# Latent attention: twelve packed query tiles, rotary rows through GpSimd and DMA copies, takes moved within each head

## The reference

```python
def mla_queries(h, w_q_a, q_a_norm, w_q_b, q_nope_norm, q_rope_norm, cos, sin):
    c_q = rms_norm(h @ w_q_a, q_a_norm)                       # 384 wide
    q = (c_q @ w_q_b).reshape(bsz, seq, 16, 96)
    q_nope = rms_norm(q[..., :64], q_nope_norm)
    q_rope = apply_rope(rms_norm(q[..., 64:], q_rope_norm), cos, sin)   # 32 wide
    return concatenate([q_nope, q_rope])
# keys: k_nope = rms_norm of 64 columns of c_kv @ w_kv_b for each head, k_rope 32 wide, shared by all heads
# causal_block_attention: softmax(q k^T / sqrt(96)) v for 16 heads of 64 value columns; then x + o @ w_o
def apply_rope(x, cos, sin):
    x1, x2 = split(x, 2)
    return concatenate([x1 * cos - x2 * sin, x1 * sin + x2 * cos])
```

## Time and profile before

| what | value |
|---|---|
| median of three runs | 1870.35 us |
| the profiled execution | 1866.67 us, span 1864.6 us |
| PE busy | 1810.5 us (97%) |
| PE weight loads | 1395.1 us (75%), beside PE |
| DVE busy | 1041.5 us (56%) |
| ACT busy | 839.4 us (45%) |
| POOL busy | 199.6 us (11%) |
| mean granted TensorE clock | 0.99 |
| chain that ended last | PE 88%, DVE 4%, ACT 3%, POOL 3%, issue 1% |

### The profile page before, as it was taken

One profiled execution on the slowest core, in us unless ns is written; L12 is line 12 of the kernel. 1 busy time (PEld: TensorE's weight loads), 2 busy tenths in 40 slices (PEclk: granted clock), 3 DMA queues, 4 the chain that ended last, 5 costly groups with the idle time before them and its releaser, 6 DMA issues.

```text
span 1864.6 us, 24367 instructions
## 1 busy us (share of the span) xinstructions
PE 1810.5 (97%) x8934; PEld 1395.1 (75%) x8934; DVE 1041.5 (56%) x1633; ACT 839.4 (45%) x1406; POOL 199.6 (11%) x269
## 2 busy tenths in 40 slices
PE   9889999999999999999999999999999989999997
PEld 6677778888887766677888888768666767866675
DVE  8874454444334767755444434465555476556647
ACT  5423344443224666644444422232567633265753
POOL 7970000000000000000000000023000012200000
PEclk9989999999999999999999999999999999999998
DMA  6322322323333111122232333323111122311111
GB/s 212 103 58 79 98 94 90 101 91 98 94 96 101 44 35 28 62 74 96 90 101 92 98 94 94 97 87 106 57 57 46 46 90 88 105 51 52 57 45 57
DMA packets 58764, 152.21 MB, mean 82 GB/s; under 512 B 17152, under 2 KB 22048, under 8 KB 58672
## 3 DMA queue, kind: packets, MB, share of 16 engines
q1 hardware_dynamic: 55120, 148.27, 25.3%
q0 software_dynamic: 3552, 2.70, 0.5%
HBM read 143.79 MB, written 4.19 MB: 79 GB/s over the span
## 4 chain that ended last, share of the span: by engine, by line
PE 88%; DVE 4%; ACT 3%; POOL 3%; issue 1%; DMA 0%; SPq 0%; DVEq 0%; ACTq 0%; POOLq 0%
PE bank L2027 19%; PE bank L2028 18%; PE bank L2029 18%; PE bank L2522 3%; PE bank L2524 3%; PE bank L2523 3%; PE bank L2499 2%; PE bank L2487 2%; PE bank L2486 2%; PE bank L2485 2%; PE bank L2254 1%; PE bank L2282 1%; PE bank L2609 1%; PE bank L2537 1%; PE bank L2506 1%
## 5 line engine op out<-in xcount | busy, mean ns | idle before, releaser
L1253 DVE TENSOR_TENSOR wl<-raw,wh 128x1024 fp32r<-128x1024 f32 (+3 forms) x280 | 324.1, 1158 | 493.9 <-ACT wh L678 490.7
L678 ACT ACTIVATE wh<-raw 128x1024 fp32r<-128x1024 f32 (+3 forms) x280 | 279.2, 997 | 573.5 <-PE bank L2029 498.0
L2027 PE MATMUL bank<-xH,wh 128*128 128x512 f32 x904 | 355.2, 393 | 3.9 <-DVE wl L1253 2.1
L2029 PE MATMUL bank<-xH,wl 128*128 128x512 f32 x904 | 352.1, 389 | 0.0
L2028 PE MATMUL bank<-xL,wh 128*128 128x512 f32 x904 | 352.1, 389 | 0.0
L2027 PEld LDWEIGHTS bank<-xH,wh 128*128 128x128 f32 x904 | 169.9, 188 | 43.4 <-DVE xL L1259 3.2
L2028 PEld LDWEIGHTS bank<-xL,wh 128*128 128x128 f32 x904 | 170.0, 188 | 35.6 <-issue 1.0
L2029 PEld LDWEIGHTS bank<-xH,wl 128*128 128x128 f32 x904 | 169.8, 188 | 35.5
L2027 PE MATMUL bank<-hidH,wh 128*128 128x512 f32 x352 | 137.3, 390 | 0.0
L2029 PE MATMUL bank<-hidH,wl 128*128 128x512 f32 x352 | 136.9, 389 | 0.0
L2028 PE MATMUL bank<-hidL,wh 128*128 128x512 f32 x352 | 136.9, 389 | 0.0
(11 more groups left out here) (450 smaller groups left out, 3305.6 us busy)
## 6 DMA issues: line engine op xcount, KB each, us to landing
raw<-w_gu_dram SPq DMA_DIRECT2D x88, 512.0 KB, 3.3
raw<-w_p_dram SPq DMA_DIRECT2D x64, 512.0 KB, 3.4
raw<-w_dn_dram SPq DMA_DIRECT2D x32, 448.0 KB, 3.3
raw<-w_glu_dram SPq DMA_DIRECT2D x16, 512.0 KB, 3.5
raw<-w_dn_dram SPq DMA_DIRECT2D x16, 512.0 KB, 3.5
raw<-w_out_dram SPq DMA_DIRECT2D x16, 512.0 KB, 3.3
raw<-w_in_dram SPq DMA_DIRECT2D x8, 512.0 KB, 7.8
raw<-w_o_dram SPq DMA_DIRECT2D x8, 512.0 KB, 3.4
```

The source lines that it names most:

```text
L678: nc.scalar.activation(wh[:, (st.base + u) % 2, 0:kts * P], raw[:, (st.base + u) % 4, 0:kts * P], ACT.Copy).then_inc(w_high, 1)
L1253: nc.vector.tensor_tensor(wl[:, s, 0:kts * P], raw[:, (st.base + u) % 4, 0:kts * P], wh[:, s, 0:kts * P].bitcast(F32), ALU.subtract).then_ ...
L2027: nc.tensor.matmul(bank, wh[:, s, w], hi[:, k, :], start=first and kt == 0, stop=False)
L2029: ins = nc.tensor.matmul(bank, wl[:, s, w], hi[:, k, :], start=False, stop=last and kt == kts - 1)
```

## The change

The sixteen query tiles become twelve: eight tiles `("n", pair)` with the 64 nope rows of two heads, and four tiles `("r", g)` with the 32 rotary rows of four heads each. VectorE takes a rotary tile into `rope_q`; GpSimd has the two halves exchanged by two DMA copies into `rope_x`, multiplies both with tables (`qtab`, filled by sixteen DMA copies), adds them, and puts the 32 rows of each head into the four buffers `qst` by four DMA copies a pair. Buffers of queries are two pairs deep now; their unused rows are set to zero. The dictionaries `MAIN` and `SECOND` say which tile is projected in which head. The keys and the nope queries are taken behind `copy_turned` and ahead of the last `row_least` of a head, and the tile of `SECOND` (heads 0, 3 and 7) behind it. The blocks of output projection at the end are placed anew. `squares_of`, `root_of`, `projected`, `mean_square` and `take` are the old helpers for any tile, and `taken_from` gives a tile's bank and place in it. The masks of the mean matmul and the order of columns in the packed weights follow.

```diff
-BLOCKS_B = [("q", 0), ("k", 0), ("v", 0), ("v", 1), ("q", 1), ("k", 1)]
-for _p in range(1, NH // 2):
-    BLOCKS_B += [("q", 2 * _p), ("q", 2 * _p + 1)] + [("k", _p + 1)] * (_p + 1 < NH // 2)
+BLOCKS_B = [("r", 0), ("k", 0), ("v", 0), ("n", 0), ("v", 1), ("k", 1), ("n", 1), ("r", 1), ("n", 2), ("k", 2), ("r", 2),
+            ("n", 3), ("k", 3), ("n", 4), ("k", 4), ("r", 3), ("n", 5), ("k", 5), ("n", 6), ("k", 6), ("n", 7), ("k", 7)]
+IN_BANK2 = [("r", 0)] + [("n", p) for p in range(NH // 2)]
+IN_BANK3 = [b for b in BLOCKS_B if b[0] != "v" and b not in IN_BANK2]
+NORMED = [b for b in BLOCKS_B if b[0] != "v"]
+MAIN = dict(enumerate([(kind, p) for p in range(2, NH // 2) for kind in "nk"], 1))
+SECOND = {0: ("r", 1), 3: MAIN[3], 7: MAIN[7]}
+MAIN.update({3: ("r", 2), 7: ("r", 3)})
...
-    qst = [mla.tensor(f"qst{b}", [P, S]) for b in range(2)]
+    qst = [[mla.tensor(f"qst{s}", [P, S])[:, :] for s in range(2)], [sq[:, s, :] for s in range(2)]]
     qtab = [mla.tensor(f"qtab{s}", [P, S]) for s in range(2)]
+    rope_q, rope_x = T[:, 1, :], sd[:, :]
...
-            pool.wait_ge(sem("hid_used0"), 1)
             pool.dma_start(posI[:, :], pos.to_broadcast([P, S])).then_inc(sem("pos_loaded"), 16)
             pool.dma_start(means[:, :], con[:, CON["mean_even"][0]:CON["fold"][1]]).then_inc(sem("means_loaded"), 16)
+            pool.wait_ge(sem("rope_table"), 1)
+            for n in range(8):
+                to = slice(n * DR // 2, (n + 1) * DR // 2)
+                turning = DN + DR + n // 4 * DR // 2
+                pool.dma_start(qtab[0][to, :], ropeT[DN:DN + DR // 2, :]).then_inc(sem("rope_rows1"), 16)
+                pool.dma_start(qtab[1][to, :], ropeT[turning:turning + DR // 2, :]).then_inc(sem("rope_rows1"), 16)
+            pool.wait_ge(sem("latnorm_ready"), KQ + KKV)
+            pool.wait_ge(sem("latroot_ready"), 3)
+            for n in range(2):
+                nc.gpsimd.memset(qst[n][0][DN + DR:P, :], 0.0).then_inc(sem("latroot_ready"), 1)
+                nc.gpsimd.memset(qst[n][1][DR:DN, :], 0.0).then_inc(sem("latroot_ready"), 1)
+            pool.wait_ge(sem("latroot_ready"), 7)
+            for g in range(NH // 4):
+                pool.wait_ge(sem("roped"), 4 * g + 1)
+                for half in range(2):
+                    pool.dma_start(rope_x[half * DN:(half + 1) * DN, :], rope_q[(1 - half) * DN:(2 - half) * DN, :])\
+                        .then_inc(sem("rope_rows0"), 16)
+                if g == 0:
+                    pool.wait_ge(sem("rope_rows1"), 256)
+                pool.wait_ge(sem("rope_rows0"), 32 * (g + 1))
+                nc.gpsimd.tensor_tensor(rope_q, rope_q, qtab[0][:, :], ALU.mult).then_inc(sem("roped"), 1)
+                nc.gpsimd.tensor_tensor(rope_x, rope_x, qtab[1][:, :], ALU.mult).then_inc(sem("roped"), 1)
+                pool.wait_ge(sem("roped"), 4 * g + 3)
+                nc.gpsimd.tensor_tensor(rope_q, rope_q, rope_x, ALU.add).then_inc(sem("roped"), 1)
+                pool.wait_ge(sem("roped"), 4 * g + 4)
+                for pair in range(2 * g, 2 * g + 2):
+                    if pair >= 2:
+                        pool.wait_ge(sem("scores_ready"), 8 * pair - 8)
+                    for s in range(2):
+                        for half in range(2):
+                            to = (DN, 0)[s] + half * DR // 2
+                            at = half * DN + (2 * (pair % 2) + s) * DR // 2
+                            pool.dma_start(qst[pair % 2][s][to:to + DR // 2, :], rope_q[at:at + DR // 2, :])\
+                                .then_inc(sem(f"rope_placed{pair % 2}"), 16)
...
-                if h + 2 < NH:
-                    query_squares(h + 2)
-                    if h + 2 < NH - 2:
-                        ahead(st, 0, AT_B["q", h + 2], True)
+                if h in MAIN:
+                    squares_of(MAIN[h])
+                    if h < NH - 5:
+                        ahead(st, 0, AT_B[MAIN[h]], True)
                 for j in range(QT):
                     if j < 3:
                         copy_turned(h, j)
                     if h + 1 < NH:
                         probs(h + 1, 1 - s, j)
-                    if j == 1 and h + 2 < NH:
-                        query_root(h + 2)
-                        if s and pair + 2 < NH // 2:
-                            key_squares(pair + 2)
-                            ahead(st, 0, AT_B["k", pair + 2], True)
-                    if j == 2 and s and pair + 2 < NH // 2:
-                        key_root(pair + 2)
+                    if j == 1 and h in MAIN:
+                        root_of(MAIN[h])
+                    if j == 1 and h in SECOND:
+                        squares_of(SECOND[h])
+                        ahead(st, 0, AT_B[SECOND[h]], True)
+                    if j == 2 and h in SECOND:
+                        root_of(SECOND[h])
                 if pair and s == 0:
                     output_high(pair - 1)
-                if NH - 2 <= h + 2 < NH:
-                    ahead(st, 0, AT_B["q", h + 2], True)
+                if NH - 5 <= h < NH - 3:
+                    ahead(st, 0, AT_B[MAIN[h]], True)
...
+            def take_rope(g):
+                bank, i = taken_from(("r", g))
+                if g:
+                    for n in range(2):
+                        dve.wait_ge(sem(f"rope_placed{n}"), 64 * g)
+                dve.wait_ge(sem("rq_ready" if bank == 2 else "rk_ready"), i + 1)
+                nc.vector.scalar_tensor_tensor(rope_q, banks[bank][:, :], tiny[:, 25:26], (R if bank == 2 else acc)[:, :], ALU.mult, ALU.mult)\
+                    .then_inc(sem("roped"), 1)
+                dve.wait_ge(sem("roped"), 4 * g + 1)
+                dve.sem_inc(sem("q_used" if bank == 2 else "kv_used"), 1)
...
-            def head_queries(h):
-                s = h % 2
-                dve.wait_ge(sem("rq_ready"), h + 1)
-                step(nc.vector.tensor_tensor(qst[s][:, :], banks[2][:, :], R[:, :], ALU.mult))
+            def take_queries(pair):
+                dve.wait_ge(sem("rq_ready"), taken_from(("n", pair))[1] + 1)
+                for s, rows in enumerate((top, bottom)):
+                    step(nc.vector.scalar_tensor_tensor(qst[pair % 2][s][rows, :], banks[2][rows, :], tiny[rows, 24:25], R[rows, :],
+                                                        ALU.mult, ALU.mult))
                 dve.sem_inc(sem("q_used"), 1)
-                nc.vector.tensor_tensor(qst[s][:, :], qst[s][:, :], qtab[s][:, :], ALU.mult).then_inc(sem("qk_ready"), 1)
-
-            def head_keys(pair):
+                dve.sem_inc(sem("qk_ready"), 1)
+
+            def take_keys(pair):
...
-            head_queries(0)
-            head_keys(0)
+            take_keys(0)
             ahead(st, 0, 2, True)
+            ahead(st, 0, 3, True)
+            take_queries(0)
+            rope_rows(1)
             row_least(0, 0)
+            ahead(st, 0, 4, True)
             row_least(0, 1)
-            rope_rows(1)
-            ahead(st, 0, 3, True)
+            ahead(st, 0, 5, True)
             row_least(0, 2)
-            ahead(st, 0, 4, True)
+            ahead(st, 0, 6, True)
             share_first(0)
-            head_queries(1)
+            take_keys(1)
             row_least(0, 3)
-            ahead(st, 0, 5, True)
-            head_keys(1)
+            take_queries(1)
...
-                if h + 2 < NH - 2:
-                    ahead(st, 0, AT_B["q", h + 2], True)
-                elif NH - 2 <= h + 1 < NH:
-                    ahead(st, 0, AT_B["q", h + 1], True)
+                if h in MAIN and h < NH - 5:
+                    ahead(st, 0, AT_B[MAIN[h]], True)
+                elif NH - 4 <= h < NH - 2:
+                    ahead(st, 0, AT_B[MAIN[h - 1]], True)
                 if h + 1 < NH:
                     row_least(h + 1, 0)
                     row_least(h + 1, 1)
@@ -1716,17 +1782,17 @@
                 share_probs(h, 3)
                 if pair and s:
                     output_low(pair - 1)
-                if s == 0 and 1 <= pair < NH // 2 - 1:
-                    head_keys(pair + 1)
-                if h + 2 < NH:
-                    head_queries(h + 2)
-                if s and pair + 2 < NH // 2:
-                    ahead(st, 0, AT_B["k", pair + 2], True)
+                if h in SECOND:
+                    ahead(st, 0, AT_B[SECOND[h]], True)
                 if h + 1 < NH:
                     row_least(h + 1, 2)
                 copy_turned(h)
+                if h in MAIN:
+                    take(MAIN[h])
                 if h + 1 < NH:
                     row_least(h + 1, 3)
+                if h in SECOND:
+                    take(SECOND[h])
...
-                    pe.wait_ge(sem("qk_ready"), h + 1)
-                    pe.wait_ge(sem("kv_used"), pair + 2)
+                    pe.wait_ge(sem("qk_ready"), pair + 1)
+                    pe.wait_ge(sem(f"rope_placed{pair % 2}"), 64 * (pair // 2 + 1))
```

(68 more changed lines are left out.)

158 lines of the change are left out of this document (80 added, 78 removed).

## The result

The changed kernel takes 1875.97 us (median of 6 runs, 1874.52 to 1877.49), the one before, measured beside it, 1868.75 (1867.55 to 1870.58). The ratio is 1.0042, interval [1.0031, 1.0052]: 7.2 us slower. The time lies inside the range of the prediction, but the forecast case, no change, did not come. The sign is that of the slower cases; of what they named, only a fall of the clock took part.

A forecast was written before the change was run, and what follows sets the result against it. TensorE, busy 97%, was taken as the bound, with VectorE's order binding after the change. Terms +4.3, -2.7, +3.4, -0.7 and -2.7 summed to +1.6 us; forecast 1871.5 us, 8-in-10 range 1857.5 to 1879.

The forecast's parts named there:

- the forecast case, no change: Whole kernel: 1871.5 us, no change that can be told; own range 1867 to 1875, chance 0.44.
- the slower cases: Rotary chain, GpSimd beside VectorE or clock falls decide: 1879, or 1876 to 1883; slower in all 0.25.
- The stalls: TensorE's idle time before first transposes: 0.6 us in a plain pair's odd head, 1.35 in its even head.
- the gap before the output product: Head 13 on: the first output matmul waits 1.6 us until the last take frees its bank.
- head 13 to the end: Stretch from head 13 on: 27.5 us against 30.2 before, a gain of 2.7.
- the rotary chain: Start: take, DMA swap, GpSimd steps, placing copies end at 651.8 us, scores start at 651.9; later groups hidden.
- heads 3 to 10: Four pairs, alternately with and without a rotary tile: +2.6, -0.9, +2.6, -0.9, together +3.4 us.
- The pairs with a rotary tile: Two pairs, rotary tile in heads 3 and 7: 21.4 us each, 2.6 more than the 18.82 before.
- The plain pairs: Steady pairs without a rotary tile: 17.9 us each, a gain of 0.9 on 18.82.
- outside the stretch nothing should move by more than 0.5: Everything outside the stretch from the first scores at 646.1 us to 811.3: moves by at most 0.5 us.
- The slower rival: Rotary chain or GpSimd's neighbourhood decides, clock falls included: 1879, or 1876 to 1883; chance 0.24.
- the first rival: TensorE stays the bound in the heads: 1856 us, with half the gain 1863; chance 0.32, the whole 0.14.

The follow-up runs named there:

- x_defer: Changed kernel with each take of nope queries moved behind the sharing of the next head: 1868.93 us, ratio 1.0003 to the kernel before.
- x_norope: Changed kernel without GpSimd's swaps, multiplications, additions and placing copies, rotary rows of the queries left zero: 1876.27 us, ratio 1.0045 to the kernel before.
- x_kearly: Changed kernel with each take of keys (even heads) moved ahead of the third row minimum: 1868.8 us, ratio 1.0004 to the kernel before.
- x_swap: Changed kernel with the tile without rotary rows first and the rotary tile second in heads 3 and 7: 1882.62 us, ratio 1.0074 to the kernel before.
- x_tail: Changed kernel with the last third of the output product in plain order, tile 0 then tile 1: 1874.75 us, ratio 1.0037 to the kernel before.
- b_late: Kernel before with only the queries' take moved to between the copy and the last row minimum: 1877.8 us, ratio 1.005.

## Why the prediction came out as it did

**How near it came.** The sum gave +1.6; the medians differ by 7.2 and the profiled spans by 10.4. The time lies in the range of 1857.5 to 1879 because the range was wide and not because the sum was right; that is luck. Two of the costs, the waits for bank 3 in heads 3, 4, 7 and 8 and the seam to the output tile, are in none of its terms.

**Right: what binds.** That VectorE's order (copy, take, minimum 3, share) would take TensorE's place was the argument, and x_defer shows it. The stalls were forecast at 0.6 and 1.35 and measured 0.51 and 1.35. First scores were forecast at 651.9 (651.74), head 1 at 671.7 (672.22), the gap before the output product at 1.6 (1.41), head 13 to the end at 27.5 (27.36).

**Right in its end, not in its middle: the rotary chain.** The swap landed sooner than the 3.2 that I took from copies of another shape: 2.3 by the table of transfers, the placements 1.8. The Trainium skill, DMA: Bandwidth & Descriptors, section "Anatomy of one DMA — SWDGE (gpsimd) path", gives about 2 us fixed; here the trace agrees with 2.3 and 1.8, and the start was bound by the take, as the prediction had worked out for this case. GpSimd's addition took 2.15 against 1.28 for the first multiplication: VectorE's weight splits (644.53, 1.45 long, and 646.53, 0.88) fell into it, and not into the multiplications. Neither mattered: the scores waited for VectorE's own take (0.37, L1727), and x_norope did without the chain at the same time.

**Wrong: heads 3 to 10, +6.7 for +3.4.** Two things. The pairs with a rotary tile were put at 21.4 and took 22.08 (689.71 to 711.79) and 23.2 (730.23 to 753.43). The step that failed is the walk of the banks: I followed VectorE's queue to the transposes, but not the product that waits for the bank which the same take gives back. In heads 3 and 7 the first product, the rotary tile, waits 1.37 for the keys' take of the head before, and the keys' of heads 4 and 8 wait 0.58 for the rotary take; x_kearly removed the first: heads 3 and 7 take 9.77 and 9.75 there, and 11.17 each in the changed kernel, and its pairs come to 20.78, 17.78, 21.00 and 17.88, where the prediction had 21.4 and 17.9. x_swap removed it too and got as much back in front of heads 4 and 8. The 2.2 that I had forecast before the transposes of heads 4 and 8 came as 1.30 and as 1.64 + 0.58. The plain pairs were put at 17.9 and took 18.4 (711.79 to 730.23) and 18.28 (753.43 to 771.71); here the mechanism was right and the size 0.4 to 0.5 short. The odd head came as walked (7.96 for 7.95), the even one took 10.48 for 9.95: its first transpose came 0.2 later, and the rest of the head, put at 7.17, took 7.5. The wait of 0.24 for ScalarE's probabilities before the third scores was in the walk (at 5.8; it came at 717.58, 5.79 into the head).

**Wrong: "outside the stretch nothing should move by more than 0.5".** 1.55 came at 819.39, from the order of the output parts (x_tail). Right behind it the matmuls at 820.87 take 0.63 instead of 0.39, and the granted clock of 815 to 830 is 0.89: with before's 1.00 over 15 us, that is 1.65 more. 1.55 + 1.65 = 3.2 makes up the 3.12. The engine had been idle 1.55 just before. x_swap has the same idle time and the fall as well (0.90 over 815 to 830); x_norope, x_defer and x_kearly have the same idle time and no such fall, so the idle time alone isn't shown to be its cause. The last 1.1 us, in the stages behind 1219 that no edit touches, stay open.

**The chances.** The slower rival had 0.24, for the rotary chain, GpSimd beside VectorE and falls of the clock. A fall did come (1.65), and one wait of 0.6 beside GpSimd. The larger part came a third way, by the walk's own mechanism with two more places where it bites. The 1856 of the first rival does not follow from the terms it names, 12.5 of work less 3 of idle time, which give 1861. The forecast's range of 1867 to 1875 was too narrow for a sum of five walked terms.

**What packing is worth.** The two halves of the change stand apart now: sixteen query tiles with early takes 1867.6 and with late ones 1877.8 (+10.2, b_late); twelve tiles with late takes 1876.0 and with takes moved and the tail in plain order 1860.6. So packing, with the takes placed well, gives 7.0 us of the 12.5 that it removes, and the place of the takes (with the tail) is worth 15. The start's +4.85 is, by its size, most of the 5.5 that is not got back; no run takes it away alone: all kernels with twelve tiles that arrived in time have their first scores at 651.7 to 652.9.

## What to carry to other kernels

When work is taken from the bound engine, walk not only to what it waits for next in the same chain but also every buffer that the moved instruction gives back: a take that is late delays the share behind it on its own queue and the next product into its bank. Put an eviction where its engine would otherwise wait: here behind the share, or ahead of minimum 2, not just ahead of the last minimum, on which the next transposes wait. A tile order that closes one gap must be checked for how many matmuls are left behind the last user of a weight buffer.

## What the hardware showed that I had not expected

The same 1.55 us of idle time at the seam to the output tile was followed by a lower granted clock in two kernels (0.89 over 815 to 830 in the changed one, 0.90 in x_swap) and by 1.00 in three others. Inside x_swap a fall came behind 3.08 us (0.79 over 704 to 712) and none behind 3.44 (matmuls of 0.39 from 750.52). A sum should hold the 1.7 us as a possible addition to such a gap, not as a certain one. The clock also differs where the code is the same: from 120 to 130 us seven kernels had 1.00 and three 0.66, and these three came 3.6 to 4.2 us later to the stage that the experiments are about.

GpSimd and VectorE slow each other here. A step of 128x512 on GpSimd took 1.28 us and, with two weight splits of VectorE in it, 2.15; a split of 128x256 on VectorE took 0.42 us with GpSimd idle and 0.86 on average with the rotary chain. TensorE noticed it once, with 0.58 us.
